# Moving the split value buffers of the down products to eight different places modulo 512 bytes

## The reference

```python
def peer_ffn(x, w_q, subkeys, u_tab, v_tab):        # 128 * 128 experts
    ...                                             # scores, top 16 of 16 x 16 candidates, for 8 heads
    gates = jax.nn.softmax(top_s, axis=-1)
    h = jax.nn.gelu(jnp.einsum('td,ted->te', xb, u_tab[eidx]))
    w = gates * h
    return jnp.einsum('te,ted->td', w, v_tab[eidx])
```

## Time and profile before

| what | value |
|---|---|
| median of 3 runs | 2199.22 us (2195.58 to 2199.95) |
| profiled execution, its own time | 2196.69 us |
| span of its trace | 2194.9 us |
| TensorE busy | 2154.5 us (98%) |
| VectorE busy | 1686.1 us (77%) |
| ScalarE busy | 1316.4 us (60%) |
| GpSimd busy | 1014.2 us (46%) |

### The profile page before, as it was taken

One profiled execution on the slowest core, in us unless ns is written; L12 is line 12 of the kernel. 1 busy time (PEld: TensorE's weight loads), 2 busy tenths in 40 slices (PEclk: granted clock), 3 DMA queues, 4 the chain that ended last, 5 costly groups with the idle time before them and its releaser, 6 DMA issues.

```text
span 2194.9 us, 45729 instructions
## 1 busy us (share of the span) xinstructions
PE 2154.5 (98%) x15517; PEld 1961.4 (89%) x15517; DVE 1686.1 (77%) x3908; ACT 1316.4 (60%) x3002; POOL 1014.2 (46%) x820
## 2 busy tenths in 40 slices
PE   8989999999999999999999999999999999999998
PEld 8879799999999877888888988999999998788887
DVE  7766489979999856666656656999799996566666
ACT  6544474557777555555566645645777765555555
POOL 6764447997777610000043344589877774000000
PEclk9999999999999999999999999999999999999999
DMA  7548554554444665555545584455444447555554
GB/s 263 161 143 326 206 179 156 171 176 156 155 159 156 206 218 182 193 194 194 193 164 180 191 362 136 166 168 171 167 155 160 156 147 246 195 192 193 194 195 135
DMA packets 112422, 409.32 MB, mean 186 GB/s; under 512 B 16553, under 2 KB 18769, under 8 KB 107089
## 3 DMA queue, kind: packets, MB, share of 16 engines
q1 hardware_dynamic: 107744, 391.45, 52.2%
q0 software_dynamic: 4528, 15.86, 2.3%
HBM read 397.11 MB, written 10.14 MB: 186 GB/s over the span
## 4 chain that ended last, share of the span: by engine, by line
PE 62%; DVE 16%; POOL 7%; issue 4%; ACT 2%; POOLq 0%; ACTq 0%; DVEq 0%
PE banks L2712 10%; PE banks L2714 10%; PE banks L2713 10%; POOL slab_ring_lo L2150 7%; DVE one_hot_gates L2458 7%; PE banks L2201 5%; PE banks L2202 5%; PE banks L2203 5%; PE banks L296 3%; PE banks L297 3%; PE banks L298 3%; DVE slab_ring_lo L272 2%; DVE expert_activations L2475 2%; PE banks L2223 1%; DVE expert_activations L2466 1%
## 5 line engine op out<-in xcount | busy, mean ns | idle before, releaser
L2150 POOL TENSOR_TENSOR slab_ring_lo<-slab_ring,u_hi 128x512 fp32r<-128x512 f32 x504 | 663.1, 1340 | 167.5 <-ACT u_hi L2255 166.7
L2201 PE MATMUL banks<-operand_hi,u_hi 128*128 128x264 f32 x2016 | 584.8, 290 | 1.6 <-POOL slab_ring_lo L2150 1.6
L2203 PE MATMUL banks<-operand_hi,slab_ring_lo 128*128 128x264 f32 x2048 | 583.3, 285 | 0.0
L2202 PE MATMUL banks<-operand_lo,u_hi 128*128 128x264 f32 x2016 | 573.5, 284 | 0.0
L272 POOL TENSOR_TENSOR slab_ring_lo<-slab_ring,slab_hi 128x512 fp32r<-128x512 f32 x162 | 216.5, 1341 | 593.7 <-ACT slab_hi L262 593.0
L2656 DVE TENSOR_TENSOR v_lo<-slab_ring,v_hi 128x512 fp32r<-128x512 f32 x508 | 350.0, 691 | 117.7 <-ACT v_hi L2616 113.0
L2712 PE MATMUL banks<-v_hi,w_hi 128*128 128x512 f32 x1000 | 391.1, 391 | 3.4 <-DVE w_lo L2652 2.2
L2714 PE MATMUL banks<-v_lo,w_hi 128*128 128x512 f32 x1000 | 389.2, 389 | 0.0
L2713 PE MATMUL banks<-v_hi,w_lo 128*128 128x512 f32 x1000 | 389.2, 389 | 0.0
L2255 ACT ACTIVATE u_hi<-slab_ring 128x512 fp32r<-128x512 f32 x504 | 317.7, 631 | 117.8 <-PE banks L2203 115.2
L2203 PEld LDWEIGHTS banks<-operand_hi,slab_ring_lo 128*128 128x128 f32 x2048 | 385.4, 188 | 0.0
(11 more groups left out here) (443 smaller groups left out, 3794.1 us busy)
## 6 DMA issues: line engine op xcount, KB each, us to landing
slab_ring<-in_u SPq DMA_DIRECT2D x256, 512.0 KB
slab_ring<-in_v SPq DMA_DIRECT2D x256, 512.0 KB
slab_ring<-in_proj SPq DMA_DIRECT2D x144, 512.0 KB
cache_k_T<-in_cache_k SPq DMA_DIRECT2D x16, 1024.0 KB, 8.7
cache_v<-in_cache_v SPq DMA_DIRECT2D x16, 1024.0 KB, 11.8
memory_T<-in_mem POOLq DMA_DIRECT2D x2, 1024.0 KB, 6.5
sample_state<-in_state POOLq DMA_DIRECT2D x8, 256.0 KB, 3.9
out_mem_k_out<-mem_k_T SPq DMA_DIRECT2D x16, 128.0 KB, 3.0
```

The lines of the kernel that those rows point to most:

```text
L2150: nc.gpsimd.tensor_tensor(step.ring_lo[:, s, g * HC:(g + 1) * HC, :], step.slab(s)[:, g * HC:(g + 1) * HC, :], part[:, buf].bitcast(F32), ...
L2201: nc.tensor.matmul(bank, part[:, buf, k, :], xh[:, c, :], start=(c == 0), stop=False)
L2202: nc.tensor.matmul(bank, part[:, buf, k, :], xl[:, c, :], start=False, stop=False)
L2203: last = nc.tensor.matmul(bank, step.ring_lo[:, s, c, :], xh[:, c, :], start=False, stop=(c == DC - 1))
```

## The change

The start of the eight buffers is no longer lifted to the place of `w_hi` modulo 512, and each buffer gets 64 bytes behind it that nobody uses, so that neighbours begin 2112 bytes apart instead of 2048. They begin at 45888 + 2112 k, for k = 0 to 3 `v_hi` and for k = 4 to 7 `v_lo`: modulo 512 at 320, 384, 448, 0, 64, 128, 192 and 256. What is computed, in which order and with which waits stays as it is.

```diff
-SAME_PLACE = 512
+APART = 64
...
-        w_at = (nc.sbuf_base + 31) // 32 * 32
         wh = step.sb("w_hi" + L, [P, 2, TP], F32R, ctx=c1)
         wl = step.sb("w_lo" + L, [P, 2, TP], F32R, ctx=c1)
-        v_at = step.operand_at + (w_at - step.operand_at) % SAME_PLACE
-        assert v_at + 2 * 4 * HALF * 4 <= step.operand_end
-        hi, lo = (nc.alloc_sbuf_tensor_at(f"v_{name}" + L, [P, 4, HALF], F32R, offset=v_at + k * 4 * HALF * 4)
+        row = HALF + APART // 4
+        assert step.operand_at + (2 * 4 * row - APART // 4) * 4 <= step.operand_end
+        hi, lo = (nc.alloc_sbuf_tensor_at(f"v_{name}" + L, [P, 4, row], F32R, offset=step.operand_at + k * 4 * row * 4)[:, :, 0:HALF]
                   for k, name in enumerate(("hi", "lo")))
```

## The result

The changed kernel takes 2215.39 us (median of 3 runs, 2213.21 to 2217.0) against 2199.22 us: ratio 1.0082, 95% interval 1.0068 to 1.0095. It is slower by about 0.8%, outside the forecast range. The profiled execution took 2217.0 us, with a span of 2215.2 us, 20.3 us more than before.

The account below looks back on a forecast made before the run. The prediction took TensorE, busy 98% of the span, to bound the kernel. Writers at nothing and 3048 matmuls at 0.8 ns less gave 2.4 us off the median 2199.22, so 2196.8 us; range 2190 to 2212 us.

Parts of the forecast that it names:

- What bounds the stage: Down products of both layers: TensorE (PE) itself sets the pace, busy 268.88 of 270 us in layer 0.
- ScalarE and VectorE at nothing: Writing v_hi and v_lo in the down products: the buffers' new places priced at nothing for both engines.
- PE's term: 3048 matmuls of the down products: overhead falls from 13.3 to 12.5 ns each, 2.4 us less in all.
- the price of mixed places: Matmul overhead when operands start in differing places: 11.5 ns, against 13.3 ns for the down products' one same place.
- the faster rival: Down products' overhead falls to that of mixed places or below: 5.5 us less, 2193.7 us; chance 0.25.
- the slower one: Down products: some new places are bad, a quarter of matmuls at 30 ns overhead, 12.7 us more, 2211.9 us; chance 0.25.
- Its sign: In the slower case, down-product steps would differ by buffer, repeating every two slabs; no size given.
- No change that shows: Likeliest case: down products' overhead stays between 11.9 and 14.7 ns, time 2194.8 to 2203.6 us; chance 0.45.
- The rule weighed: PE's operand reads at SBUF: by the skill page's rule the sum would be nothing and the time 2199.2 us.

Follow-up runs that it names:

- all_256_off: Against the kernel before, all eight buffers start 256 bytes beyond the weights' place modulo 512; 2197.19 us beside 2196.67 us.
- all_160_off: Against the kernel before, all eight buffers, still 2048 bytes apart, start 160 bytes beyond the weights' place modulo 512; 2217.43 us, ratio 1.0098.
- both_moved: Against all_160_off, buffers unchanged, weights w_hi and w_lo moved up 160 bytes to the buffers' place modulo 512; 2195.96 us, ratio 0.9999.
- lo_128_off: Against the kernel before, v_lo starts 128 bytes beyond the weights' place modulo 512, v_hi stays at it; 2206.07 us beside 2196.67.

## Why the prediction was wrong

**What bounds the stage:** right. PE is full before and after, and 19.2 of the 20.3 us are in the two stages with the 3048 matmuls.

**ScalarE and VectorE at nothing:** right; their medians moved by 4 and 1 ns, downwards, and no new wait of PE appeared (0.3 us on v_lo in the run).

**The sign and size of PE's term:** wrong, and this is the step that failed. The prediction took the price of mixed places, 11.5 ns, from the memory projection and the up products, streams of 256 and 264 columns, and moved it to matmuls of 512 as if it were a cost of each loading of weights. In the runs it isn't: 160 bytes off costs 10.7 ns at 256 columns, less than the same place's 13.3, and 21.1 at 512; the other wrong places cost 15.6 to 20.0 at 512. It is the same-place price that is equal at 256 and 512. Nor was the memory projection as mixed as it was taken to be: its moving operands (64) lie 256 bytes from `slab_hi` (320), which all_256_off shows to be no offset at all, so that only the third matmul, with `slab_ring_lo` (128), is off, by 64. The term was forecast at 0.8 ns less per matmul and measured 7.0 ns more; 3048 x 7.8 ns = 23.8 us of difference by that count. The prediction had said of the faster rival that "their matmuls are twice as long, and the overhead may not be of place", and gave the length no term of its own.

**The rivals:** the slower one (0.25) came closest, with 2211.9 us, but by another mechanism, and its nearness is luck. It wanted two bad places of eight; in the runs each place other than a multiple of 256 bytes off costs 2 to 8 ns more per matmul at 512 columns, and all eight of the change are such places. Its price came from a rounding too: the 0.14 us step of the earlier trace rows is 133 ns in the trace's own nanoseconds, 23 over its columns and not 30, and with that the rival's sum would be 762 x 9.7 ns = 7.4 us, 2206.6 us. Its sign came true, steps that repeat every two slabs; but all_160_off has uneven steps with all buffers in one place, so this sign doesn't tell its mechanism from others. "No change that shows" rested on the even rhythm before, which speaks for one relation of places and says nothing of others. The range ended at the slower rival's own value; a bad price for all eight places, instead of two, would have reached far beyond it.

**The rule weighed:** by the Trainium skill's page SBUF — State Buffer (section "Who interferes with whom") TensorE waits for no other engine at SBUF and has separate read ports for weights and moving operand, which made the sum nothing. The runs differ: all_160_off and both_moved have the same buffers, engines and work, and 234.4 against 226.7 ns, for no more than where the weights lie. That the other engines' writing has a part in it is not shown; nor is the mechanism at the ports. Two things stay open: what in the reading makes a wrong place dearer with more columns, and what decides which of its rhythms a stream falls into, as in lo_128_off.

No version here beats the kernel before. The 512-column stream stands best at a multiple of 256 bytes, where it was; none went below its 13.3 ns. Of other streams only this can be said: cut to 256 columns the down products gained 11.6 us from being off, so lifting the 256- and 264-column streams to one place would not be expected to help; it wasn't tried.

## What to carry to other kernels

In a stream of fp32r matmuls of 512 columns with a new weight load for each, place the moving operands so that they begin a multiple of 256 bytes from the weights; it is free and was worth 0.8% here (1.0% against all_160_off). At 256 columns the same placing lost (against 160 off, the one offset tried), so measure at the length that the stream has: an overhead per matmul read from a shorter stream can't be moved to a longer one. When two matmul streams are compared, read start to start over a hundred steps; PE's busy share says 98% either way.

## What the runs showed that was not expected

The same place costs exactly as much at 256 as at 512 columns: 120.0 - 106.7 and 226.7 - 213.3 are both 13.3 ns, 32 periods of 2.4 GHz. Being 160 off costs 10.7 and 21.1 ns. The period is 256 bytes and sharp: 8 bytes off give 233.3 ns, and 64 is the only cheap offset of those tried (228.9, in one layer). A mismatch in one product of three can make the other two long as well, and whether it does can change within one layer, at a pause in the stream.
